# A hybrid attention layer on one core: the first norm's weight spread by TensorE, the bias line's load in pieces, and the second norm's root applied at the up eviction

## The reference

```python
def hybrid_layer(h, p, t5_table):
    xn = rms_norm(h, p["g_pre_mix"])
    z = xn @ p["w_in"] + p["b_in"]
    ...                                   # z is split into three mixers and their gates
    y_a = gla_branch(...) @ p["w_br_gla"]
    y_b = dsa_branch(...) @ p["w_br_dsa"]  # its logits add a bias line, t5_table by distance
    y_c = mlstm_branch(...) @ p["w_br_ml"]
    mix = sigmoid(gate_a) * y_a + sigmoid(gate_b) * y_b + sigmoid(gate_c) * y_c
    h = h + rms_norm(mix @ p["w_out"], p["g_post_mix"])
    xn = rms_norm(h, p["g_pre_mlp"])
    u = square(relu(xn @ p["w_up"]))
    return h + rms_norm(u @ p["w_down"], p["g_post_mlp"])
```

## Time and profile before

| | |
|---|---|
| median of 3 runs | 1341.84 us (1340.75 to 1343.14) |
| the profiled execution, its own time | 1341.9 us |
| its span, first to last instruction | 1340.1 us |
| TensorE busy | 1291.8 us (96%) |
| GpSimd busy | 779.4 us (58%) |
| VectorE busy | 618.9 us (46%) |
| ScalarE busy | 387.4 us (29%) |
| mean granted TensorE clock | 0.991 |

### The profile page before, as it was taken

The page is one execution under the profiler, slowest core; times in us unless marked ns, Lnnn a source line. Parts: engine busy times, 40 slices in busy tenths (PEclk is TensorE's granted clock), DMA queues, the critical chain, the costliest instruction groups (busy, mean ns, idle before and its releaser), DMA issues.

```text
span 1340.1 us, 17178 instructions
## 1 busy us (share of the span) xinstructions
PE 1291.8 (96%) x6445; PEld 1039.6 (78%) x6448; DVE 618.9 (46%) x1114; ACT 387.4 (29%) x787; POOL 779.4 (58%) x918
## 2 busy tenths in 40 slices
PE   6999989999999999999989999999899999999997
PEld 4866777766898788777888888788688888888886
DVE  3236797783146666652274563241711112333334
ACT  4243334444002333234023333221501111222322
POOL 8366431042654545455755556587567777888882
PEclk9999899999999999999999999999999999999999
DMA  7963210041322212222334333252133333222221
GB/s 180 213 221 97 71 32 16 18 126 48 94 71 72 63 48 64 63 63 64 95 95 107 91 95 87 77 189 95 48 95 94 95 95 110 94 95 94 95 79 63
DMA packets 168440, 121.08 MB, mean 90 GB/s; under 512 B 12264, under 2 KB 146510, under 8 KB 168358
## 3 DMA queue, kind: packets, MB, share of 16 engines
q1 hardware_dynamic: 161654, 108.84, 28.4%
q10 hardware_dynamic: 6704, 11.15, 2.6%
HBM read 115.72 MB, written 9.62 MB: 94 GB/s over the span
## 4 chain that ended last, share of the span: by engine, by line
PE 84%; DVE 8%; DMA 3%; ACT 2%; issue 1%; POOL 1%; SPq 0%; DVEq 0%; ACTq 0%; POOLq 0%
PE GP L1730 41%; PE PA L1765 8%; PE GP L1765 7%; PE GP L1745 7%; PE GP L1727 4%; DMA wraw<-in_w_in 3%; PE GP L1931 2%; PE PA L1888 2%; PE PA L2069 2%; PE PA L1967 1%; PE PA L1980 1%; PE PA L1911 1%; DVE S L1229 1%; POOL wlo L605 1%; DVE top L1228 1%
## 5 line engine op out<-in xcount | busy, mean ns | idle before, releaser
L605 POOL TENSOR_TENSOR wlo<-wraw,whi 128x256 fp32r<-128x256 f32 x712 | 577.2, 841 | 14.8
L601 POOL TENSOR_SCALAR whi<-wraw 128x1024 fp32r<-128x1024 f32 x178 | 194.8, 1094 | 518.8 <-PE GP L1730 251.7
L1730 PE MATMUL GP<-xh,whi 128*128 128x512 f32 x368 | 154.3, 419 | 3.4 <-DVE xl L1180 1.4
L1730 PE MATMUL GP<-xh,wlo 128*128 128x512 f32 x368 | 147.0, 400 | 0.0
L1730 PE MATMUL GP<-xl,whi 128*128 128x512 f32 x368 | 147.0, 399 | 0.0
L1683 DVE TENSOR_TENSOR ul<-U,uh 128x512 fp32r<-128x512 f32 x64 | 65.5, 1059 | 106.6 <-ACT uh L1110 106.6
L1730 PE MATMUL GP<-nh,whi 128*128 128x512 f32 x256 | 102.6, 401 | 0.7 <-DVE nl L1667 0.7
L1730 PE MATMUL GP<-nl,whi 128*128 128x512 f32 x256 | 102.4, 400 | 0.0
L1730 PE MATMUL GP<-nh,wlo 128*128 128x512 f32 x256 | 102.3, 400 | 0.0
L1687 DVE TENSOR_TENSOR U<-U 128x512 f32<-128x512 f32 x32 | 34.7, 1084 | 145.4 <-ACT U L1114 145.4
L1730 PEld LDWEIGHTS GP<-xh,whi 128*128 128x128 f32 x368 | 70.5, 192 | 22.3 <-issue 4.1
(11 more groups left out here) (373 smaller groups left out, 2701.8 us busy)
## 6 DMA issues: line engine op xcount, KB each, us to landing
wraw<-in_w_in SPq DMA_DIRECT2D x75, 512.0 KB, 3.8
wraw<-in_w_up SPq DMA_DIRECT2D x32, 512.0 KB, 4.0
wraw<-in_w_down SPq DMA_DIRECT2D x32, 512.0 KB, 3.5
line_rows<-bias_line SPq DMA_DIRECT2D x1, 5240.0 KB, 26.6
table<-line_rows SPq DMA_DIRECT2D x1, 4096.0 KB, 14.6
wraw<-in_w_br_dsa SPq DMA_DIRECT2D x8, 512.0 KB, 4.0
wraw<-in_w_br_gla SPq DMA_DIRECT2D x8, 512.0 KB, 3.9
wraw<-in_w_br_ml SPq DMA_DIRECT2D x8, 512.0 KB, 3.9
```

The source lines that it names most:

```text
L601: nc.gpsimd.tensor_scalar(hi, src, 1.0, 1.0, ALU.mult, ALU.mult).then_inc(hi_done, 1)
L605: part = nc.gpsimd.tensor_tensor(lo[:, at:to], src[:, at:to], hi[:, at:to].bitcast(FP32), ALU.subtract)
L1730: ins = mm(ps[0:t.m, 0:SEQ], wt[:, s0, w], av, start=st, stop=sp_)
```

## The change

Three parts.

**First, the input stage.** `gbc` and its DMA go. ACT loads the weight row (4 KB) into partition 0 of `grow`, whose other rows POOL and DVE have zeroed, and PE multiplies a matrix of ones by it into `GP[1]`, 512 columns at a time. DVE reads the weight from there. PE runs 13 matmuls of ones by ones ahead of it and 11 more between the transposes (`warm`). `cq0` and `cq1` are emitted in pieces of 256 tokens (`half`): the high-weight part of `cq0` for tokens 0 to 255 stands ahead of the last tile's transposes, and the high-weight part of `cq1` needs only `hi_done` and stands behind the meta tokens' transposes without waiting for their split. DVE negates and copies the bias line, which ACT did. The 29 small DMAs become 23. The meta tokens' transposes go to `PA[1]`.

**Second, the bias line.** The repeat is eight DMAs of 16 copies, ahead of chunks 6 to 13, and the read back four DMAs of four heads, ahead of chunks 14 to 17.

**Third, the second norm.** DVE multiplies `hf` 0 of the projection by its weight beforehand, adds the residual with one operation for it, and writes `xn` as the residual times the weight, without the root. ACT makes a diagonal matrix `dg` of each tile's roots, PE multiplies ones by it, so that `rrow` holds the root of every token along the columns, and DVE applies `max(up, 0) * rrow` when it empties each `up` product; ACT squares it. `transposed(0)` and `transposed(1)` move into the middle of tiles 2 and 3 of `out`, and `up0` and `up1` are emitted in halves of 256 tokens.

```diff
@@ SP @@
-                if t == 0:
-                    sp.dma_start(gbc[:, :], a["g_pre_mix"].broadcast_to([P, D])).then_inc(ld_pre, 16)
...
-                if c["r"] == 6:
+                if 6 <= c["r"] < 14:
                     sp.wait_ge(line_out, 16)
-                    sp.dma_start(scratch[:, :, 0:LINE], line.unsqueeze(0).broadcast_to([P, DSA_H, LINE])).then_inc(line_rep, 16)
-                if c["r"] == 14:
-                    sp.wait_ge(line_rep, 16)
-                    sp.dma_start(table[:, :, :], ...).then_inc(table_in, 16)
+                    r_ = 16 * (c["r"] - 6)
+                    sp.dma_start(scratch[r_:r_ + 16, :, 0:LINE], line.unsqueeze(0).broadcast_to([16, DSA_H, LINE])).then_inc(line_rep, 16)
+                if 14 <= c["r"] < 18:
+                    sp.wait_ge(line_rep, 16 * 8)
+                    h_ = 4 * (c["r"] - 14)
+                    sp.dma_start(table[:, h_:h_ + 4, :], ...).then_inc(table_in, 16)
@@ POOL @@
+            nc.gpsimd.memset(grow[:, 0:3 * D // 4], 0.0).then_inc(grow_zero, 1)
@@ ACT @@
+            act.dma_start(t5[:, :], a["t5_bias"]).then_inc(ld_line, 16)
+            act.wait_ge(grow_zero, 2)
+            act.dma_start(grow[0:1, :], a["g_pre_mix"]).then_inc(ld_pre, 16)
             act.dma_start(oh[:, :], a["onehot"]).then_inc(ld_line, 16)
-            act.dma_start(t5[:, :], a["t5_bias"]).then_inc(ld_line, 16)
...
-                if t == 3:
-                    act.wait_ge(line_ps, 1)
-                    nc.scalar.activation(rline[:, 0:LINE], GP[0][0:DSA_H, 0:LINE], ACT.Copy, scale=-1.0).then_inc(line_ok, 1)
...
+            def residual(t):
+                act.wait_ge(h_ok, 2 * t + 1)
+                seq(first_half(1, t, hres[:, t, 0:SEQ]))
+                if t == QT - 1:
+                    high_norm(t)
+                act.wait_ge(h_ok, 2 * t + 2)
+                seq(root(1, t, hres[:, t, SEQ:D]))
+                nc.scalar.activation(dg[:, t, :], ident[:, :], ACT.Copy, scale=ssf[:, 1, t, 0:1]).then_inc(dg_ok, 1)
+            projected(0)
+            projected(1)
+            residual(0)
+            high_norm(0)
+            projected(2)
+            residual(1)
+            high_norm(1)
+            projected(3)
+            residual(2)
+            high_norm(2)
+            residual(3)
...
-                ps = ready(f"up{m}")
-                nc.scalar.activation(U[:, m, :], ps[:, 0:SEQ], ACT.Relu).then_inc(gfree[tl[f"up{m}"].slot], 1)
+                whole(f"up{m}")
+                nc.scalar.activation(U[:, m, :], U[:, m, :], ACT.Square).then_inc(U_ok, 1)
@@ DVE @@
+                if t == 1:
+                    dve.wait_ge(line_ps, 1)
+                    ts(rline[:, 0:LINE], GP[0][0:DSA_H, 0:LINE], -1.0, None, ALU.mult).then_inc(line_ok, 1)
...
-            def scaled_norm(t):
-                dve.wait_ge(o_ss, 2 * t + 2)
+            def residual_scaled(t):
+                dve.wait_ge(o_ss, t + 1)
+                dve.wait_ge(g0_ok, t + 1)
                 for hf in range(2):
-                    c = slice(hf * SEQ, (hf + 1) * SEQ)
-                    stt(xn[:, t, c], hres[:, t, c], ssf[:, 1, t, 0:1], gains[:, 1, c], ALU.mult, ALU.mult).then_inc(n_ok, 1)
+                    c, ps = slice(hf * SEQ, (hf + 1) * SEQ), accumulators("out", hf, t)
+                    if hf == 0:
+                        stt(hres[:, t, c], ps, ssf[:, 0, t, 0:1], hres[:, t, c], ALU.mult, ALU.add).then_inc(h_ok, 1)
+                    else:
+                        seq(stt(ps, ps, ssf[:, 0, t, 0:1], gains[:, 0, c], ALU.mult, ALU.mult))
+                        tt(hres[:, t, c], ps, hres[:, t, c], ALU.add).then_inc(h_ok, 1)
+                    dve.wait_ge(h_ok, 2 * t + hf + 1)
+                    tt(xn[:, t, c], hres[:, t, c], gains[:, 1, c], ALU.mult).then_inc(n_ok, 1)
...
-                whole(f"up{m}")
-                tt(U[:, m, :], U[:, m, :], U[:, m, :], ALU.mult).then_inc(U_ok, 1)
+                ps = ready(f"up{m}")
+                stt(U[:, m, :], ps[:, 0:SEQ], 0.0, rrow[:, :], ALU.max, ALU.mult).then_inc(gfree[tl[f"up{m}"].slot], 1)
@@ PE, start @@
+            pe.wait_ge(ones_ok, 1)
+            warm(13, PA[1][:, 0:P])
+            pe.wait_ge(ld_pre, 16)
+            pe.wait_ge(grow_zero, 2)
+            for c in (slice(0, SEQ), slice(SEQ, D)):
+                mm(GP[1][:, c], ones[:, :], grow[:, c], start=True, stop=True).then_inc(gain_ps, 1)
+            warm(4, PA[1][:, 0:P])
+            pe.wait_ge(masks, 1)
+            transposed_in(0)
...
-            pe.wait_ge(xl_ok, KT)
-            pe.wait_ge(line_ok, 1)
-            gemm("cq0")
+            pe.wait_ge(xl_ok, 4)
+            pe.wait_ge(hi_done, 1)
+            half("cq0", 0, high, True, False)
+            transposed_in(3)
+            pe.wait_ge(split_done, 1)
+            half("cq0", 0, low, False, True)
+            pe.wait_ge(xl_ok, KT)
+            half("cq0", 1, high, True, False)
+            half("cq0", 1, low, False, True).then_inc(gemm_done, 1)
@@ PE, around the second norm @@
-            for t in range(QT - 2, QT):
-                transposed(t)
-            pe.wait_ge(nl_ok, 2 * QT - 1)
-            gemm("up0", 0)
-            pe.wait_ge(nl_ok, 2 * QT)
-            gemm("up0", 1)
-            for m in range(1, FT):
+            transposed(2)
+            pe.wait_ge(nl_ok, 4)
+            half("up0", 0)
+            transposed(3)
+            pe.wait_ge(nl_ok, 6)
+            half("up1", 0)
+            pe.wait_ge(nl_ok, 8)
+            half("up0", 1).then_inc(gemm_done, 1)
+            pe.wait_ge(dg_ok, QT)
+            for t in range(QT):
+                ins = mm(accumulators("out", 0, 0)[:, t * P:(t + 1) * P], ones[:, :], dg[:, t, :], start=True, stop=True)
+            ins.then_inc(rr_ps, 1)
+            half("up1", 1).then_inc(gemm_done, 1)
+            for m in range(2, FT):
```

More of the change, by code:

```diff
@@ L104, in row_sources @@
     return [((0, 0), part)]
-NROWDMA = 29
+NROWDMA = 23
 SMALL = [C_IW, C_GA, C_MI, C_MF]
@@ L1123, in _ @@
                 act.wait_ge(tok_done, QT + t + 1)
-                root(2, t, accumulators("down", 1, t))
+                root(2, t, accumulators("down", 1, t)).then_inc(o_ss, 1)
         @block.vector
@@ L1769, in token_gemm, with transposed_in @@
                 return ins
[L1772 to L1777 removed]
+            def transposed_in(t):
                 pe.wait_ge(xn_ok, t + 1)
```

142 lines of the change are left out of this document (92 added, 50 removed).

## The result

The changed kernel takes 1328.11 us (median of 4 runs, 1325.88 to 1331.66), the kernel before beside it 1341.68 us (4 runs, 1340.75 to 1343.14): a ratio of 0.989, 95% interval 0.988 to 0.991, 13.6 us less. The profiled execution took 1331.66 us for a span of 1329.9.

The account below looks back on a forecast made before the run. PE, busy 96% of the span, was taken to bound the kernel by its waits and slow pace. Input stage 7.2, bias line 1.2 and second norm 6.9 sum to 15.3 us: 1341.9 to 1326.6 us, range 1323 to 1331.5.

Parts of the forecast that it names:

- the first case: Whole kernel: the three gains come as summed, 1326.6 us, own range 1324 to 1328.5; chance 0.60.
- `ik` 7.2 us earlier, at 29.2: Input stage: first matmul of `ik` at 29.2 instead of 36.4, with PE at the upper clock level; 7.2 us gained.
- DVE's last `xl` ends at about 19.7: Input stage: DVE's last `xl` ends at about 19.7 us, not 20.4.
- Chunk 6, 1.2 us: Bias line: in pieces ahead of chunks 6 to 13, PE's wait for chunk 6's split goes; 1.2 us gained.
- The remark beside it: Bias line: with `ik` 7.2 us earlier, an unsplit DMA would be only partly earlier, so the wait wouldn't stay 1.2.
- the 3.3 and 3.65: Bias line DMAs: 3.3 us for each 0.65 MB repeat piece; 14.6 / 4 us for each 1 MB table piece.
- The second norm, 6.9 us: Second norm: shorter DVE chain, with PE doing halves of `up0` and `up1` meanwhile; `up2` at 977.1 instead of 983.98, 6.9 us.
- the third rival: Second norm: the clock falls in the two remaining gaps, costing 2.5 to 4 us; 1329 to 1330.6, chance 0.15.
- What is earlier stays earlier: Between the places: nothing else limits, as DVE waits 16.46 us for PE before the first logits and POOL mostly for PE's buffers.
- The table isn't late: First logits: the table's last piece, asked for at about 105, there at 109, at worst 105 + 14.6; needed from 132.
- the fifth rival: First logits: the table, its last piece asked for with chunk 17, is late and DVE waits; slower, 1345, chance 0.03.
- The rule that the prediction set against the change: Input stage and second norm: PE idling between bursts drops to its lower rate; at worst both places lose their full-rate halves.

Follow-up runs that it names:

- e6_order: Changed kernel with the transposes of input tile 3 ahead of the first half of `cq0` instead of behind it; 1329.99 us.
- e12_filled: Changed kernel with ones in later PE waits, 9 instead of 13 before the weight, `cq0`'s first half split around tile 3's transposes; 1324.47 us.
- e3_nowarm: Changed kernel without the 24 matmuls on ones in the input stage that no result is read from; 1329.9 us.

## Why the prediction was right, step by step

The forecast was 1326.6 us with a range of 1323.0 to 1331.5; 1328.11 was measured, and the first case (as summed) is what happened. Its own range, 1324 to 1328.5, held too, though by 0.4 us and with some luck: of the four executions two took 1325.9 and 1326.0, two 1330.2 and 1331.7, and the slowest lies outside the whole range. The sum was 15.3 us, measured were 13.6.

- **`ik` 7.2 us earlier, at 29.2.** It came at 30.11, and at 29.7 as the mean of seven profiles, against 36.4 and 36.8: 6.9 us by the means. The upper level held, as forecast. Two steps were off. The weight's row was there at 5.4, not at 6.4, but thirteen ones stand in front of its matmuls until 5.6 to 7.0, so it didn't matter. And "DVE's last `xl` ends at about 19.7" was 20.55: I let tile 3's transposes run when `X` was ready (17.0), though in the program they stand behind the first half of `cq0` until 17.99, and ACT waited for them. `e6_order` and `e12_filled` showed that this order can't simply be turned round, only split.
- **Chunk 6, 1.2 us.** The term was read from one execution, and another of the same code and DMA had no such wait, so it is anything from 0 to 1.2. The remark beside it was worth more than the term: that it wouldn't have stayed 1.2 with `ik` earlier. Unsplit it costs 5.9 us. The pieces took 5.3 us each from issue to landing, not the 3.3 and 3.65 that came of dividing the whole; no wait hung on that.
- **The second norm, 6.9 us.** Undisturbed it gave 47.9 - 40.9 = 7.0 us, and the steps fit by the same marks: DVE's last tile starts 25.7 us behind the first square (forecast 961.75 - 936.04 = 25.7), its five operations take 4.4 us (4.5), `up2` comes at 40.9 (41.1). What it was to be charged for, the third rival, happened in 3 of 8 profiled executions, the changed kernel's own among them (0.21 us between the matmuls of `up1`'s first half until 966.0), at 1.5 us each and not 2.5 to 4, since the pace came back after some 3.3 us.
- **What is earlier stays earlier.** Right: DVE waits 16.46 us for PE before the first logits in both kernels, the parts add within their intervals, and from `ik` to the first square the profiles with the change take 898.3 to 901.4 us (905.6 with the big DMA, less with the waits filled), 899.6 before.
- **The table isn't late.** DVE has no wait on it before the first logits; the fifth rival had nothing in it.
- **The clock behind gaps.** The granted clock fell in 28 of 36 cases at three places with waits of 0.4 to 1.9 us, and in none of 6 where these were filled; elsewhere it held behind like waits in most executions. The rule that the prediction set against the change (Trainium skill, "TensorE: Matmul & The Clock Gate", "HAM oscillation — how this bites in real kernels") is that a PE that idles in gaps drops to its lower rate and pays to come back. The trace agrees in direction, not for every gap, and behind isolated waits that are shorter than those of the page's example. The rule bore on parts of this kernel to which I hadn't applied it.

In sum the missing 1.7 us are 0.3 to 0.5 at the input stage, 1.2 or less at chunk 6, and 1.5 x 3/8 = 0.6 for the clock in the second norm. How they share the rest isn't settled, since the executions of one kernel spread by more than that.

## What to carry to other kernels

Before a stage is shortened, look at the transfer behind it: a DMA that cost 1.2 us at most would have cost 5.9 with the stage in front shortened. Where an engine's operand becomes unnecessary (here the root before the transposes), the gain can lie in the order that this allows, not in the operation, so price the queue of the engine that made it: under the changed kernel's order the root in front cost 12.6 us, under the order of before its price was not measured. Where PE is busy for 98%, its remaining waits of 1 to 2 us can cost twice, once as a wait and once as the pace behind it: a few matmuls without a use in the wait, never ahead of real ones, took 2.7 to 3.2 us out of the stretch between `ik` and the first square here. With the split of `cq0` and the second norm's wait filled too, the whole gave 3.6. Where another engine is late next, less comes of it.

## What the runs showed of the hardware

I had taken the granted clock to be steady on one core outside the two places. It isn't: the same code fell at two to four of these places in one execution and at others in the next, 1.6 to 3.4 us of PE's time each, of which as little as 0.3 us was left behind the next wait. That does not explain the larger part of the spread between runs. Two executions of the changed kernel with the same mean granted clock, 0.993, took 1325.88 and 1330.23 us, and in `e6_order` all five have 0.993 and lie between 1326.18 and 1330.34. What makes that difference stays open. In the first 7 us the moment at which the pace doubles also differed from one execution to the next, by 1.4 us at the weight's matmuls, with nothing but the same ones on PE. The record doesn't show it: over the first 10 us of the changed kernel its granted clock is 1.00, and over 5.40 to 9.13 us of `e3_nowarm` too, where four passes of 512 columns took 3.73 us, twice what the upper level gives (1.91 for those at 6.95 in the changed kernel).
